# A hybrid decoder kernel: router on unscaled rows, positions in bf16, pair tables behind the first gather

## The reference

```python
def rmsnorm(x, g):
    x32 = x.astype(jnp.float32)
    y = x32 * lax.rsqrt(jnp.mean(x32 * x32, axis=-1, keepdims=True) + RMS_EPS)
    return (y * g.astype(jnp.float32)).astype(x.dtype)

def hier_moe(xn, w_rg, b_rg, w_re, b_re, w_gu, w_dn):
    ...
    lg = jnp.dot(xf, w_rg).astype(jnp.float32) + b_rg.astype(jnp.float32)
    grp = jnp.argmax(lg, axis=-1)
    ...
    le = (jnp.dot(xf, w_re).astype(jnp.float32) + b_re.astype(jnp.float32)).reshape(n_tok, N_GROUPS, EXPERTS_PER_GROUP)
    le = jnp.take_along_axis(le, grp[:, None, None], axis=1)[:, 0]
    top_p, top_e = lax.top_k(jax.nn.softmax(le, axis=-1), EXPERT_TOP_K)
    gate = p_grp_sel * top_p / jnp.sum(top_p, axis=-1, keepdims=True)
    ...
    gu = lax.ragged_dot(xs, w_gu, sizes)
    g_, u_ = jnp.split(gu, 2, axis=-1)
    ys = lax.ragged_dot(jax.nn.silu(g_) * u_, w_dn, sizes)
    ys = ys * gate.reshape(-1)[order][:, None].astype(ys.dtype)
    return jnp.zeros_like(xf).at[tok_s].add(ys).reshape(B, T, D)
```

## Time and profile before

| | us |
|---|---|
| median of 3 runs | 1445.12 (1444.04 to 1446.16) |
| profiled execution, its own time | 1444.26 |
| its span | 1442.1 |
| PE busy | 1243.6 |
| PE weight loads busy (beside PE) | 739.3 |
| DVE busy | 496.2 |
| ACT busy | 243.4 |
| GpSimd busy | 81.2 |

### The profile page before, as it was taken

How to read it: one execution, slowest core, us unless ns; L and a number is a source line. 1 busy time by engine, 2 the same in 40 slices (tenths; PEclk the granted TensorE clock), 3 DMA queues, 4 the chain that set the end, 5 groups by cost and what they waited for, 6 DMA issues and landing times.

```text
span 1442.1 us, 26136 instructions
## 1 busy us (share of the span) xinstructions
PE 1243.6 (86%) x10690; PEld 739.3 (51%) x10690; DVE 496.2 (34%) x1113; ACT 243.4 (17%) x564; POOL 81.2 (6%) x105
## 2 busy tenths in 40 slices
PE   4989898699899898878889889969988998798885
PEld 3877756444444343434468776655444443344332
DVE  4254634433223222322242654353223232222323
ACT  2003213011111111111120221221111111111111
POOL 1121300000000000000021222000000000000000
PEclk9999999699999999999999999979999999999997
DMA  8231229299999999999944113567999999999993
GB/s 337 93 147 59 102 82 428 81 426 428 427 386 428 428 427 427 428 428 429 423 174 166 60 59 117 246 279 298 425 428 385 428 429 427 429 427 427 429 428 147
DMA packets 33103, 455.11 MB, mean 316 GB/s; under 512 B 3744, under 2 KB 4000, under 8 KB 5152
## 3 DMA queue, kind: packets, MB, share of 16 engines
q1 hardware_dynamic: 33056, 454.46, 75.4%
HBM read 453.40 MB, written 1.05 MB: 315 GB/s over the span
## 4 chain that ended last, share of the span: by engine, by line
PE 48%; DMA 39%; DVE 6%; ACT 2%; issue 2%; SPq 1%; DVEq 0%; ACTq 0%
PE bank L459 47%; DMA share<-in_w_gu 30%; DMA share<-in_w_dn 9%; SPq L370 1%; ACT xnT L1044 1%; DVE small L1469 1%; PE bank L518 1%; DMA lb_in<-in_lb_logits 1%; DVE share L1449 1%; PE bank L677 1%; DVE rest L1760 0%; DVE h L1401 0%; ACT ring L1098 0%; DVE rest L1690 0%; ACT xhat L1025 0%
## 5 line engine op out<-in xcount | busy, mean ns | idle before, releaser
L459 PE MATMUL bank<-share,rest 128*32 128x512 f32 (+1 forms) x2560 | 309.6, 531 | 16.5 <-DMA share<-in_w_dn 16.4
L459 PE MATMUL bank<-ring,rest 128*32 128x256 f32 (+1 forms) x1792 | 184.5, 492 | 35.9 <-DMA share<-in_w_gu 30.4
L459 PE MATMUL bank<-dense,rest 128*32 128x256 f32 (+2 forms) x1824 | 190.3, 480 | 24.6 <-DMA share<-in_w_gu 21.9
L459 PE MATMUL bank<-xnT,dense 128*128 128x256 f32 (+2 forms) x960 | 162.4, 344 | 13.4 <-ACT xnT L1044 6.3
L459 PEld LDWEIGHTS bank<-share,rest 128*32 128x32 f32 x2560 | 102.7, 113 | 111.7 <-issue 94.8
L459 PEld LDWEIGHTS bank<-xnT,dense 128*128 128x128 f32 (+1 forms) x960 | 140.5, 179 | 32.2 <-issue 13.3
L459 PE MATMUL bank<-rest 96*128 96x512 f32 (+1 forms) x288 | 122.0, 579 | 34.3 <-DVE rest L1760 34.3
L459 PEld LDWEIGHTS bank<-ring,rest 128*32 128x32 f32 x1792 | 66.7, 113 | 156.0 <-issue 98.8
L1751 DVE TENSOR_TENSOR rest<-rest,bank 64x512 f32<-64x512 f32 x64 | 35.7, 558 | 322.3 <-ACT rest L1175 296.0
L459 PEld LDWEIGHTS bank<-dense,rest 128*32 128x32 f32 (+1 forms) x1824 | 69.6, 112 | 146.5 <-issue 97.8
L459 PE MATMUL bank<-rest,xhat 128*128 128x96 f32 x1088 | 142.2, 286 | 2.7 <-DVE rest L1679 2.7
(11 more groups left out here) (229 smaller groups left out, 954.9 us busy)
## 6 DMA issues: line engine op xcount, KB each, us to landing
share<-in_w_dn SPq DMA_DIRECT2D x64, 2048.0 KB, 19.8
ring<-in_w_gu SPq DMA_DIRECT2D x48, 2048.0 KB, 23.7
dense<-in_w_gu SPq DMA_DIRECT2D x48, 2048.0 KB, 26.6
share<-in_w_gu SPq DMA_DIRECT2D x32, 2048.0 KB, 22.9
dense<-in_w_units SPq DMA_DIRECT2D x18, 2048.0 KB, 9.0
dense<-in_w_units SPq DMA_DIRECT2D x4, 1024.0 KB, 5.1
dense<-in_w_units SPq DMA_DIRECT2D x2, 1184.0 KB, 5.8
ring<-in_w_units SPq DMA_DIRECT2D x2, 1024.0 KB, 5.8
```

What stands on the lines that cost most here:

```text
L459: return pe.matmul(out_ap, lhsT=lhsT, rhs=rhs, start=start, stop=stop, skip_group_check=True)
```

## The change

- The transposes ahead of the router read h in place of xhat. Those of tile 0 stand ahead of `cross_out(1)` in PE's queue and go through the banks 4 and 5; router group 0 stands behind `cross_out(1)`, then come the transposes and the group of tile 1. The root of the mean square is multiplied to the logits on DVE, one operation per tile, with the bias.
- ACT scales both tiles into xhat after its evictions; DVE no longer scales tile 1. The first gather waits for both.
- `chosen`, the triangle and the ones are bf16. The latter two come with the masks and are cast with them.
- DVE evicts the first gather as soon as the number of passes is written; the pair tables follow behind it. GpSimd's product of layer 0 waits for the second pair's gated one-hot.

```diff
@@ USES, bank 4 and 5 @@
-    4: ["hq", "hidT", "rk", "cmp_t"] + [f"t{n}_0" for n in range(NG)],
+    4: ["hq", "hidT", "rk", "cmp_t"] + [f"t{n}_0" for n in range(NG)] + ["zT0"],
@@ setup @@
-            sp.dma_start(rest[:, 0:1312], masks).then_inc(s_setup, 16)
+            sp.dma_start(rest[:, 0:1568], masks).then_inc(s_setup, 16)
-            V.tensor_copy(cbf[:, :], rest[:, 1024:1312]).then_inc(ev("masks"), 1)
+            V.tensor_copy(cbf[:, :], rest[:, 1024:1568]).then_inc(ev("masks"), 1)
@@ TensorE @@
+                turn("z", "ffn", 0, h)
                 cross_out(1)
-
                 bk = bank_free(pe, l, "rt")
-                for tt in range(2):
-                    turn("z", "ffn", tt)
+
+                def route(tt):
                     settled(f"zT{2 * tt}", f"zT{2 * tt + 1}")
                     for k in range(8):
                         ins = mm(bk[:, tt * 36:(tt + 1) * 36], xnT[:, k, tt * P:(tt + 1) * P],
                                  pcol(l, RW + k * 36, 36), k == 0, k == 7)
-                bank_done(ins, "rt")
+                    return ins
+
+                route(0)
+                turn("z", "ffn", 1, h)
+                bank_done(route(1), "rt")
...
-                mm(bk[:, 0:E], tri, chosen[:, 0, :], True, True)
+                mm(bk[:, 0:E], tri_b, chosen_b[:, 0, :], True, True)
...
+                wait("xhat0_ffn")
+                wait("xhat1_ffn")
                 gather(0, 0)
@@ ScalarE @@
                 norm("ffn", 0)
+                turned("z", G_FFN, 0)
                 norm("ffn", 1)
-                turned("z", G_FFN, 0)
                 turned("z", G_FFN, 1)
+                for tt in range(2):
+                    wait(f"rstd{tt}_ffn")
+                    act.activation(xhat[:, tt, :], h[:, tt, :], ACT.Identity,
+                                   scale=rs[:, tt:tt + 1]).then_inc(ev(f"xhat{tt}_ffn"), 1)
@@ GpSimd @@
-                    wait("npass_ready")
+                    pool.wait_ge(pg_of[l], 2)
+                    alone(pool)
                     gained(xnT[:, :, :], l + 1).then_inc(ev("memG"), 1)
@@ VectorE @@
+                turned("z", G_FFN, 0)
                 norm("ffn", 0)
                 add_out("co", "ffn", 1)
-                turned("z", G_FFN, 0)
+                turned("z", G_FFN, 1)
                 norm("ffn", 1)
-                turned("z", G_FFN, 1)
...
-                bank_drained(V.tensor_tensor(rl, bk[:, 0:72].rearrange("p (t c) -> p t c", t=2),
-                                             bc(pcol(l, RBIAS, 36).unsqueeze(1), 2, 36), ADD), "rt")
+                for tt in range(2):
+                    ins = V.scalar_tensor_tensor(rl[:, tt, :], bk[:, tt * 36:(tt + 1) * 36], rs[:, tt:tt + 1],
+                                                 pcol(l, RBIAS, 36), MUL, ADD)
+                bank_drained(ins, "rt")
...
                 own("npass_ready", V.tensor_copy(npass_i[0:1, 0:1], r_np[0:1, :]))
+                gathered(0)
                 link(V.tensor_scalar(r_pos, r_pos, -1.0, None, ADD))
...
-                gathered(0)
                 with dve.Fori(0, npass * PAIRS) as t:
```

More of the change, by code:

```diff
@@ L51 @@
     3: ["xT0", "hf", "ksvs", "cmpo", "cmp_s_1"] + [f"s{n}_1" for n in range(NG)],
-    4: ["hq", "hidT", "rk", "cmp_t"] + [f"t{n}_0" for n in range(NG)],
-    5: ["ckv", "rq0"] + [f"t{n}_1" for n in range(NN)] + ["hot"] + [f"t{n}_1" for n in range(NN, NG)],
+    4: ["hq", "hidT", "rk", "cmp_t"] + [f"t{n}_0" for n in range(NG)] + ["zT0"],
+    5: ["ckv", "rq0"] + [f"t{n}_1" for n in range(NN)] + ["hot"] + [f"t{n}_1" for n in range(NN, NG)] + ["zT1"],
     6: ["q0", "rq1", "o6", "xo0", "rt"],
@@ L104, in hymba @@
         cst = sb("cst", [P, consts.shape[1]])
-        cbf = sb("cbf", [P, 288], BF16)
+        cbf = sb("cbf", [P, 544], BF16)
+        chosen_b = sb("chosen_b", [P, 2, 32], BF16)
         lvmask = sb("lvmask", [P, 8, 128], U8)
@@ L137, in hymba @@
         cmp_no_b = cbf[:, 256:288].rearrange("p (t c) -> p t c", t=2)
+        tri_b = cbf[:, 288:416]
+        ones_b = cbf[:, 416:544]
         def pcol(l, a, n):
@@ L220, in rtile @@
             return ys_b[:, at:at + 2 * n].rearrange("p (t c) -> p t c", t=2)
-        rl, rlog, r_in, r_o1, r_o2, chosen = [
-            rtile(a, n) for a, n in ((0, 36), (72, 36), (144, 32), (272, 32), (336, 32), (400, 32))]
+        rl, rlog, r_in, r_o1, r_o2 = [
+            rtile(a, n) for a, n in ((0, 36), (72, 36), (144, 32), (272, 32), (336, 32))]
         rexp = rtile(464, 36)
@@ L509, in two_N, with turn @@
                     bank_done(ins, use)
-                def turn(prefix, stage, tt):
-                    wait(f"xhat{tt}_{stage}")
+                def turn(prefix, stage, tt, rows=xhat):
+                    wait(f"xhat{tt}_{stage}" if rows is xhat else f"h{tt}_{stage}")
                     for j in range(2):
@@ L517, in turn @@
                             k = 4 * j + d
-                            ins = pe.transpose(bk[:, d * P:(d + 1) * P], xhat[:, tt, k * P:(k + 1) * P], ident)
+                            ins = pe.transpose(bk[:, d * P:(d + 1) * P], rows[:, tt, k * P:(k + 1) * P], ident)
                         bank_done(ins, f"{prefix}T{tt * 2 + j}")
@@ L1034, in norm @@
                     squares(stage, tt).then_inc(ev(f"squares{tt}_{stage}"), 1)
-                    if tt == 0:
+                    if tt == 0 and stage != "ffn":
                         wait("rstd0_" + stage)
@@ L1384, in norm @@
                     own(f"rstd{tt}_{stage}", inverse_root(link, rs[:, tt:tt + 1], ssq[:, tt:tt + 1], 1.0 / D))
-                    if tt == 1:
+                    if tt == 1 and stage != "ffn":
                         V.tensor_scalar(xhat[:, 1, :], h[:, 1, :], rs[:, 1:2], None,
@@ L1657, in _ @@
                 first_of_max(r_e2, r_in, iota_e, 32, r_o2)
-                own("chosen", V.tensor_tensor(chosen, r_o1, r_o2, ADD))
+                V.tensor_tensor(chosen_b[:, :, :], r_o1, r_o2, ADD).then_inc(ev("chosen"), 1)
                 V.tensor_tensor(rlog[:, :, 0:4], lg, bc(r_mg.unsqueeze(2), 2, 4), SUB)
@@ L1693, in _ @@
                 bk = bank_full(dve, l, "pos")
+                wait("chosen")
                 link(V.scalar_tensor_tensor(r_pos, bk[:, 0:2 * E].rearrange("p (t e) -> p t e", t=2), 1.0,
-                                            chosen, ADD, MUL))
+                                            chosen_b[:, :, :], ADD, MUL))
                 bank_drained(V.tensor_copy(r_cnt, bk[:, 2 * E:3 * E]), "pos")
@@ L1716, in _, with gathered @@
                 own("npass_ready", V.tensor_copy(npass_i[0:1, 0:1], r_np[0:1, :]))
+                def gathered(n):
+                    for b in range(2):
+                        dve.wait_ge(efilled[b], n + 1)
+                        g = bc(pcol(l, G_FFN + 4 * b, 4).unsqueeze(2), 4, ROWS)
+                        V.tensor_tensor(xg[:, 4 * b:4 * b + 4, :], banks[b][:, 0:4 * ROWS].rearrange("p (d s) -> p d s", d=4),
+                                        g, MUL).then_inc(edrained[b], 1)
+                gathered(0)
                 link(V.tensor_scalar(r_pos, r_pos, -1.0, None, ADD))
@@ L1729, in _ @@
                 npass = dve.value_load(npass_i[0:1, 0:1], min_val=1, max_val=MAXP)
-                def gathered(n):
-                    for b in range(2):
-                        dve.wait_ge(efilled[b], n + 1)
-                        g = bc(pcol(l, G_FFN + 4 * b, 4).unsqueeze(2), 4, ROWS)
-                        V.tensor_tensor(xg[:, 4 * b:4 * b + 4, :], banks[b][:, 0:4 * ROWS].rearrange("p (d s) -> p d s", d=4),
-                                        g, MUL).then_inc(edrained[b], 1)
-                gathered(0)
                 with dve.Fori(0, npass * PAIRS) as t:
@@ L1811, in constants @@
     bf = np.concatenate([
-        eye, np.where(p[None, :] > p[:, None], -1e30, 0.0), (1.0 - ok.reshape(P, 32)) * -1e30], axis=1)
+        eye, np.where(p[None, :] > p[:, None], -1e30, 0.0), (1.0 - ok.reshape(P, 32)) * -1e30,
+        (p[:, None] < p[None, :]), np.ones((P, P))], axis=1)
     s, t = p[:, None], p[None, :]
```

8 lines of the change are left out of this document (4 added, 4 removed), and 4 rows, old and new, of the table USES.

## The result

The changed kernel took 1423.99 us (median of 4 runs, 1421.55 to 1425.39) beside 1445.64 us for the kernel before (4 runs, 1444.04 to 1446.56). The ratio is 0.985, with an interval of 0.9833 to 0.9867: 21.7 us less, with 19.2 to 24.1 us inside the interval. The profiled execution took 1423.51 us, its span is 1421.6.

What follows compares the result with a forecast made beforehand. Bound: the chain of waits through pair 0 of the expert loop, then the expert weight transfers. Layer 0 10.85 plus layer 1 5.4 less setup 0.45 gives 15.8 us gained: 1429.3 us from the 1445.12 median, range 1424.3 to 1435.5.

Steps and rivals of the forecast that it cites:

- The stream follows pair 0: Expert loop: whatever brings pair 0 forward brings the weight stream's restart and its end forward by as much.
- the 1.8 us: Layer 0, pair 0 to last transfer: pair 0 at full clock gains 1.8 us, from 430.32 − 428.51; bounds 0 and 1.8.
- the 428.5 us in both layers: Sign to check: the weight stream's length from pair 0; any other length in either layer would show the prediction wrong.
- Router: Last heads to router logits: reordered transposes and groups gain 5.1 us a layer; bounds 2.5 and 6.8.
- For group 1 I take the slow 3.60.: Tile 1's router group: taken at half clock, 3.60 us, so it ends at 251.35 in place of 256.45.
- The projection is pushed to 239.6 to 243.3.: Second tile's output projection, layer 0: 0.65 us later behind tile 0's transposes; router group 0 follows at 243.4.
- Positions: Positions after the router's choice: bf16 makes 10 matmul records 5 and removes DVE's wait, gaining 0.4 us a layer.
- Tables: Pair tables behind the first gather's eviction: pair 0 starts 3.65 us earlier in layer 0, nothing gained in layer 1.
- Setup: Kernel start: larger mask transfer (0.31 us) and larger bf16 cast (0.14) lose 0.45 us, once.
- Rival B: Clock stays up through both router groups, gathers quicker by up to 0.7 each: gain 20.6 us, 1424.5; chance 0.13.
- Rival A: Clock takes the gain: router groups, tile 1's transposes and layer 0's pair 0 slow; gain 8.8 us, 1436.3; chance 0.16.

Runs made afterwards that it cites:

- router alone: The kernel before with only the diff's router part (transposes of h, tile 0's ahead of the projection, root put into the logits); 1433.18 us, ratio 0.9918.
- late cast: The changed kernel with the bf16 triangle and ones cast from f32 constants behind the first products, mask transfer at its old size; ratio 0.9845.
- the kernel with added products: The changed kernel plus constant bf16 products: 5 ahead of the second router group, 20 behind it, 9 behind the positions; 1418.59 us, ratio 0.9817.
- the run without the first piece: The changed kernel plus 20 constant products behind the second router group and 9 behind the positions, none ahead of that group; ratio 0.9837.

## Why the prediction was wrong

**The stream follows pair 0: right, but the 1.8 us is in part luck.** Pair 0 came 8.79 us earlier in layer 0 and the last transfer 10.58 us earlier, a difference of 1.79 us, forecast as 1.8. The pieces of the chain don't bear the agreement out. Before (first row) and after (the other two):

```profile
404.41 5.40 PE bank L459 x64
...
266.91 12.48 PE bank L462 x144
...
392.93 7.10 PE bank L462 x64
```

Pair 0 itself ran at full clock and took 12.48 us in place of 14.69, 2.2 us less. But a later piece of 64 products, between two transfers, took 7.10 us in place of 5.40 and gave 1.7 back, and another 1.3 us of gain is as little explained as the 1.13 of layer 1. The prediction took the difference of two lengths of one profile for the price of the clock. In the 14 profiles this length is 426.9 to 430.6 us where pair 0 ran at full clock, and 430.1 to 431.0 in the three with a slow pair 0; the 428.5 us in both layers, which the prediction asked for, came as 428.53 and 427.38. The Trainium skill's remark that the activity watch is free-running (TensorE: Matmul & The Clock Gate, Part 1) fits, and by much more than the 0.4 us of the earlier trace rows: the same second router group took 3.60 us in one layer and 1.95 in the other in three kernels, and the slow layer was layer 0 in one of them and layer 1 in two.

**Router: mechanism right, size wrong.** This is the step that failed. The term was 5.1 us a layer; it measured 6.97 and 7.15, together 3.9 of the 4.7 us by which the profiles gained more than the sum. (The sum took the rows of layer 0 for both layers; layer 1 had 0.35 us less to lose, 18.76 us against 19.11.) Two steps of it failed.
- "For group 1 I take the slow 3.60." In the kernels with the new router and no product added ahead of this group, the ten groups of five profiles (the changed kernel twice, router alone, late cast, added products behind the group) took 2.47, 1.95, 1.95, 3.60, 3.60, 1.95, 3.02, 2.69, 1.95 and 3.60 us, a mean of 2.7. In the changed kernel's first profile it was 2.47 and 1.95, 1.1 and 1.65 us under the term; that both layers fell on the quick side there is luck. I took the worst case as the likeliest, on the ground that no row showed such a group at full clock. But in the rows of before PE idled for 0.88 us ahead of the warm transposes and for over 1.5 us behind them; in the new order it works for over 8 us ahead of tile 1's eviction. A likely reason, then, is the work ahead of the group, and the runs with five products ahead of this group support it. But the same work stood ahead of all ten groups, and six of them still lost the clock; why one does and another doesn't is not shown. The 1.87 us of group 0 was forecast as 1.9.
- "The projection is pushed to 239.6 to 243.3." Counted from the last heads, the projection ended 5.55 us behind them and not 5.9, and group 0 overlapped its end: it was done at 7.26 us, not at 7.9. I summed the lengths of rows that stand apart before, where in an unbroken queue each row starts 0.07 to 0.17 us ahead of the end of the one before it. That is 0.7 us a layer, and 0.8 by the start of the second group.

With the mean of 2.7 us and these 0.8 the forecast would have been some 3.4 us lower, at 1425.9; the remaining 1.9 us is of the size of the slow spells below.

**Positions: right.** 0.32 us a layer with the second root operation in it, against 0.3. DVE's wait is gone; alone the part gives 0.5, and the extra root operation costs 0.18 (8.73 us from logits to gather in the router alone against 8.55), not 0.1.

**Tables: right, with one effect too many.** 4.05 us in layer 0 against 3.65 (the gather was 0.4 quicker by its clock). What the prediction didn't say is that either of the two edits alone does it. GpSimd's product moved as forecast, with a stall of 3.4 us under its cover:

```profile
294.19 3.60 POOL L1225 TENSOR_TENSOR xnT<-memT,par 128x2048 f32<-128x2048 f32 x1 [125.39 <-DVE rest L1758]
294.24 3.76 DVE L1695 TENSOR_TENSOR rest<-cst,posv 128x192 f32<-128x192 f32 x1 [0.20 <-DVE rest L1758]
```

**Setup: right.** 0.65 us lost in this pair of profiles, and 0.46 between the means of all 14, against 0.45.

**What had no term.** Slow spells (stretches in which the same products take longer, at half clock) outside the change: one in attention of layer 0 (−1.90) and the last pair of layer 0 (+1.73). The 14 profiles show 33.8 to 33.9 us from the last transfer to the end in six and 35.4 to 35.5 in eight, whatever the kernel. The 80 products behind the last transfer of layer 0 took 7.32 us in eight profiles and 9.02 in the other six. So the end of either layer has one of two lengths, 1.7 us apart. The 1.13 us of layer 1's stream wasn't explained. Together the three are 1.0 us of this pair of profiles. Spells of this size are a likely reason for runs of one kernel that lie 4 us apart. The mean granted clock of each run supports it in part: of the 11 runs with the bf16 positions alone, the three at 0.956 took 1439.9 to 1440.4 us and the five at 0.949 and 0.950 took 1444.0 to 1445.3; but the kernel with added products took 1415.4 to 1419.4 us at 0.971 or 0.972 in every run.

Rival B (the clock stays up, 1424.5) was nearest in its number, with 0.13, but its condition held only in part: the second group kept the full clock in four of ten cases, and the gathers took 5.72 and 6.75 us and not 0.7 less than before. Rival A was given more, though its slow first group came in none of the 18 cases of the nine profiles with the new order, 1.87 us each. On these counts B deserved more than A.

## What to carry to other kernels

Where a chain of short products decides when a weight stream starts, write the queue so that TensorE goes from one to the next without idling: moving eight transposes ahead of a projection was worth 5 of 7 us a layer here, with a queue on DVE that was written for that order. If the engine idles there anyway, constant products into a bank that is overwritten later kept the clock, where they stood on both sides of the second group, and gained another 5.5 us; more of them in every pair gained nothing and made the early pairs 1.5 us longer. A term that is the difference of two lengths of one profile should be checked against its pieces: here it agreed to 0.01 us, partly by luck. Price a group whose clock isn't known by both levels, and keep the worse for the range and not for the sum.

## What was not expected of the hardware

- A 36-column router group of 16 records took 1.87 to 1.95 us at full clock and 3.60 at half. In the kernel before the granted clock stayed at 0.50 through the second group, PE busy all along; during the gather, and during the added products of the run without the first piece, it came back to 1.00. In the changed kernel it fell within the second group of layer 0, some 1.2 us after its start (1.00 in 249.4 to 250.2, 0.82 in 250.2 to 251.0, 0.50 in 251.0 to 252.0), with no idle time of PE longer than 1.39 us since the last heads.
- A bf16 product 128x512 took 0.22 us in a row of 20 at full clock. The five bf16 position products took 0.31 us in all, where the ten f32 records had taken 2.34 us, both at a granted clock of 0.50.
- A DVE operation with one operand in PSUM ran at 0.56 us beside GpSimd's 3.60 us product. One with both operands in SBUF ended only with that product, after 3.56 us before and 3.76 after, in place of 0.23 and 0.36.
